# The mask and row-decay additions of a DeltaNet head's exponent table, moved from GpSimd to VectorE

## The reference

```
gc = cumsum(g)                                  # per chunk
decay[i, j] = exp(gc[i] - gc[j])  for j <= i,  else 0
lower = strict_tril(beta * (k k^T) * decay)
sol = inverse(I + lower) @ [v*beta, k*beta*exp(gc)]
qk = tril((q k^T) * decay)
per chunk: o = q_dec S + qk v_new ;  S = S*exp(g_last) + k_dec^T v_new
```

## Time and profile before

| | |
|---|---|
| median of the runs | 1423.48 us |
| the profiled execution's own time | 1425.28 us |
| its span | 1423.6 us |
| mean granted TensorE clock in it | 0.987 |
| PE busy | 94% of the span |
| DVE busy | 56% |
| ACT busy | 48% |
| POOL busy | 20% |

### The profile page before, as it was taken

How to read it: one execution, slowest core, us unless ns; L and a number is a source line. 1 busy time by engine, 2 the same in 40 slices (tenths; PEclk the granted TensorE clock), 3 DMA queues, 4 the chain that set the end, 5 groups by cost and what they waited for, 6 DMA issues and landing times.

```text
span 1423.6 us, 25677 instructions
## 1 busy us (share of the span) xinstructions
PE 1337.1 (94%) x9981; PEld 984.1 (69%) x9981; DVE 803.6 (56%) x2210; ACT 680.7 (48%) x1757; POOL 284.4 (20%) x206
## 2 busy tenths in 40 slices
PE   5999999999999998499999999999999999998998
PEld 4866766667544456388777877788778787875543
DVE  6235444444354426867578576675776775852243
ACT  6155464554555425246465463664654736543121
POOL 7211021110011143304122141131220413200000
PEclk9999999999999999799999999999999999999999
DMA  5011010020211111011021110110111101034121
GB/s 184 31 44 31 15 45 16 30 75 30 89 60 60 73 60 47 30 46 31 17 65 41 35 56 17 46 45 32 60 31 46 46 16 61 1 137 175 30 74 74
DMA packets 19416, 74.81 MB, mean 53 GB/s; under 512 B 3040, under 2 KB 3296, under 8 KB 17760
## 3 DMA queue, kind: packets, MB, share of 16 engines
q1 hardware_dynamic: 19296, 73.18, 15.0%
HBM read 61.04 MB, written 12.12 MB: 51 GB/s over the span
## 4 chain that ended last, share of the span: by engine, by line
PE 70%; DVE 14%; ACT 9%; issue 4%; DMA 2%; POOL 1%; SPq 0%; POOLq 0%; DVEq 0%; ACTq 0%
PE bank L1629 16%; PE bank L1726 12%; PE bank L1701 8%; PE bank L1766 4%; PE bank L1656 4%; PE bank L1682 3%; PE bank L1741 3%; PE bank L1667 3%; DVE arena L1531 2%; PE bank L1900 2%; PE bank L1914 2%; PE bank L1825 2%; PE bank L1917 2%; DVE arena L1391 2%; DVE arena L1533 2%
## 5 line engine op out<-in xcount | busy, mean ns | idle before, releaser
L1726 PE MATMUL bank<-hn_hi,w_hi 128*128 128x512 f32 x512 | 225.6, 441 | 17.5 <-ACT arena L1049 17.5
L1726 PE MATMUL bank<-hn_hi,w_lo 128*128 128x512 f32 x512 | 203.8, 398 | 0.0
L1726 PE MATMUL bank<-hn_lo,w_hi 128*128 128x512 f32 x512 | 203.0, 397 | 0.0
L1629 PE MATMUL bank<-hn_hi,w_hi 128*128 128x512 f32 x320 | 136.8, 428 | 0.5 <-ACT arena L984 0.3
L916 POOL TENSOR_TENSOR w_lo<-arena,w_hi 128x1024 fp32r<-128x1024 f32 x30 | 76.7, 2557 | 298.8 <-ACT w_hi L1080 298.8
L1629 PE MATMUL bank<-hn_hi,w_lo 128*128 128x512 f32 x320 | 125.9, 394 | 0.0
L1629 PE MATMUL bank<-hn_lo,w_hi 128*128 128x512 f32 x320 | 125.8, 393 | 0.0
L1726 PEld LDWEIGHTS bank<-hn_hi,w_hi 128*128 128x128 f32 x512 | 98.3, 192 | 36.4 <-ACT arena L1049 20.4
L1701 PE MATMUL bank<-arena 128*128 128x512 f32 x256 | 119.0, 598 | 0.0
L1726 PEld LDWEIGHTS bank<-hn_hi,w_lo 128*128 128x128 f32 x512 | 97.8, 191 | 22.7
L1263 DVE CUSTOM_DVE_ANT_0 arena<-bank,arena 128x384 f32<-128x384 f32 (+1 forms) x128 | 70.1, 582 | 67.0 <-issue 66.7
(11 more groups left out here) (231 smaller groups left out, 2670.8 us busy)
## 6 DMA issues: line engine op xcount, KB each, us to landing
arena<-in_w SPq DMA_DIRECT2D x52, 512.0 KB, 3.6
arena<-in_x SPq DMA_DIRECT2D x16, 512.0 KB, 4.5
arena<-gc_scratch SPq DMA_DIRECT2D x8, 1024.0 KB, 5.0
x_scratch<-arena SPq DMA_DIRECT2D x8, 512.0 KB, 2.6
arena<-x_scratch SPq DMA_DIRECT2D x8, 512.0 KB, 3.7
out<-arena SPq DMA_DIRECT2D x8, 512.0 KB, 2.6
oT_scratch<-arena SPq DMA_DIRECT2D x7, 512.0 KB, 4.9
arena<-oT_scratch SPq DMA_DIRECT2D x7, 512.0 KB, 8.1
```

The source lines that it names most:

```text
L1629: ins = te.matmul(bank[r % 2][:], wp[:, tile % 2, k], hp[:, k, hf * HALF:(hf + 1) * HALF], start=(k == 0 and m == 0), stop=(k == KT - 1 an ...
L1726: ins = te.matmul(b[:], wp[:, t % 2, k], hp[:, k, hf * HALF:(hf + 1) * HALF], start=(k == 0 and m == 0), stop=(k == KT - 1 and m == 2))
```

## The change

The event list stays as it is. The `etm` event is taken out of the POOL program and put into the DVE program. DVE executes the same two additions for each direction, in its own order, directly behind `tab1` and ahead of everything else that follows in the list. `link` makes the next DVE instruction wait for the completion of this one.

```diff
--- before.py
+++ after.py
@@ -914,13 +914,6 @@
                     t = e[1]
                     pool.wait_ge(w_rounded, t + 1)
                     gp.tensor_tensor(w_lo[:, t % 2], ring1[:, t % 2], w_hi[:, t % 2].bitcast(F32), ALU.subtract).then_inc(w_split, 1)
-                elif e[0] == "etm":
-
-                    h, d = e[1], e[2]
-                    pool.wait_ge(tab_dve, h * 3 + 1)
-                    gp.tensor_tensor(ET[:, d], ET[:, d], bc(emask[:, d], NT), ALU.add).then_inc(pch, 1)
-                    pool.wait_ge(pch, 8 + 2 * h + d)
-                    gp.tensor_tensor(ET[:, d], ET[:, d], bc(head_tab2[:, h % 2, 2, NT * d:NT * d + NT], P, 2), ALU.add).then_inc(et_masked, 1)
                 elif e[0] == "diag":
@@ -1376,6 +1369,12 @@
                     link(ve.memset(invT, 0.0))
+                elif e[0] == "etm":
+
+                    h, d = e[1], e[2]
+                    dve.wait_ge(tab_dve, h * 3 + 1)
+                    link(ve.tensor_tensor(ET[:, d], ET[:, d], bc(emask[:, d], NT), ALU.add))
+                    ve.tensor_tensor(ET[:, d], ET[:, d], bc(head_tab2[:, h % 2, 2, NT * d:NT * d + NT], P, 2), ALU.add).then_inc(et_masked, 1)
                 elif e[0] == "conv":
```

## The result

The changed kernel takes 1458.66 us (median of four runs, 1456.56 to 1459.61) against 1423.86 for the kernel before on the same chip. The ratio is 1.0238, with a 95% interval of 1.0217 to 1.0260. The change makes the kernel 34.8 us slower. The forecast was 1466, in a range of 1440 to 1473.

What follows compares the result with a forecast made beforehand. PE was taken to stall behind DVE's late gate eviction: 32.4 (PE's loss) + 10.2 (clock) + 0.8 (head 1) - 0.9 (head 0) = +42.5 us, giving 1466.0 for the median, range 1440 to 1473.

Steps and rivals of the forecast that it cites:

- What bounds: Behind the small table, DVE has 1.29 us of room before the gate eviction L1471, then PE's key transposes stop.
- Duration of the additions: Four 128x1024 additions per head on DVE, 1.22 us each, bounds 0.745 and 1.285.
- The collision: At the shared SBUF port POOL's L916 goes ahead of DVE's fourth addition, which ends at 928.07 instead of 925.85.
- the other order: DVE's fourth addition gets the port before POOL's L916; L1471 3.60 us late, total 1451; chance 0.27.
- What PE loses: Key transposes 5.82 us later, less 0.42 taken up at L1860 and L1818: 5.40 per head, 32.4 over six head changes.
- The clock: PE's granted clock falls behind each 6 us stall, costing 1.7 us at six heads, 10.2 in all.
- Head 0: DVE's constant chain: 4.85 of additions plus 1.3 of collision less 7.1 no longer lost to POOL's masks, -0.9 us.
- Head 1: No gate eviction; POOL goes before the third addition and the state copies reach PE's L1799 late, +0.8 us.
- DVE first at the port: Rival: the fourth addition precedes L916, 3.18 us net lost per head, clock falls at five of six; 1451; chance 0.27.
- The cheap case: Rival: additions of 0.745 us, giving 1429, or a held clock, giving 1443 or 1456; chance 0.13.
- The freed port: Rival: DVE no longer stands still behind POOL's masks, so the kernel gets faster, about 1419; chance 0.05.
- No change: Rival: the table is not on the bound path, delays are taken up before the inversion; 1423.5; chance 0.05.

Runs made afterwards that it cites:

- pool-waits kernel: Changed kernel, but POOL waits at each head until both directions are masked, so L916 cannot run beside the fourth addition; 1447.24 us, ratio 1.0161.
- 24 fillers: Changed kernel with 24 extra 128x128 matmuls, results unused, on PE ahead of the key transposes of heads 2 to 7; 1450.34 us, ratio 1.0180.
- 48 fillers: Changed kernel with 48 extra 128x128 matmuls, results unused, on PE ahead of the key transposes of heads 2 to 7; 1477.31 us, ratio 1.0369.
- woven: Changed kernel with DVE's additions placed one by one into gaps around the gate eviction and state copies, and POOL's L916 held back; 1421.85 us, ratio 0.9985.

## Why the prediction was right

*What bounds.* Shown. DVE's gate eviction became the wait in front of PE six times, and moving the additions behind it took four fifths of the loss away.

*Duration of the additions.* 1.22 was taken. Measured 1.22 (medians 1.224 and 1.225).

*The collision.* Predicted 3.4 for the fourth addition and L1470 "some 7 us behind the table"; measured 3.38 and 6.99. POOL won the port at each of the six heads, as the sum said with a margin of some 0.03. The sum took each addition from bounds of 0.745 to 1.285, so it couldn't decide an order by that margin; that it named the right one was luck. The prediction itself gave the other order 0.27. The pool-waits kernel priced the collision at 11.4 us in all.

*What PE loses.* Here two terms were mis-sized. The transposes were to be 5.82 later and are 5.51 later. In before they waited for ACT's silu, not for the eviction, which had some 0.2 of room, and the eviction moved by 5.70. And 0.42 was to be taken up behind them. The 24 fillers give 5.51 - (97.63 - 93.30) = 1.18, the 48 fillers 1.38. The two places were right and their sizes wrong: I had read the idle time of PE's matmuls there, 0.17 and 0.25, and not that of the weight loads ahead of them. These rows of before are the same instructions on PEld:

```profile
925.92 1.86 PEld L1860 LDWEIGHTS bank<-arena 128*128 128x128 f32 x16 [0.36 <-ACT arena L1101]
...
933.04 0.71 PEld L1818 LDWEIGHTS bank<-arena 128*128 128x128 f32 x4 [0.68 <-ACT arena L1066]
```

They sum to 1.04. Followed from matmul to matmul, from the table's start in before and in 24 fillers (the head at 920.78 and 930.27), PE's delay is 5.51 at the first key transpose and 5.69 at the fifth. It is 5.46 at the end of the first L1818 group, 5.03 two matmuls into L1860, and 4.41 behind the first matmuls of the next L1818. Then it stands at 4.33. Three other heads give the same as far as there.

*The clock.* It fell at all six heads. Priced at 1.7 from a window of before, measured at 1.48. The sum for one head is 5.51 - 1.18 + 1.48 = 5.81, the same as 99.11 - 93.30; it must be, since 1.18 and 1.48 were themselves got as differences of these periods. 7.1 was predicted. The 1.3 of difference over six heads is 7.8 us. In the profiled spans the difference is 31.2 where 42.5 was predicted, 11.3 less: about 7.8 from here, 2 from the last head and 1.2 from head 1. The medians are 34.8 apart, 3.6 more than the spans. No term of the sum foresaw that, and it brings the forecast that much nearer by luck.

*The last head.* Six heads were counted alike, but the last one gained back about 2 us: 226.56 - 222.82 = 3.74. In the final stretch of before the granted clock fell behind a 2.8 us stall; in after it stayed at 1.00 there. Before's row, and the one of after that answers to it, in windows of 5 us:

```profile
1295.00:1300.00 5.00, 5.00 (x18) 3.51 (x17) 1.50 (x2) 1.62 (x5) 0.00 (x0) 0.66 0.09 36
```

```profile
1327.00:1332.00 5.00, 5.00 (x25) 3.09 (x24) 1.67 (x4) 1.91 (x5) 0.00 (x0) 1.00 0.12 51
```

Whether this comes with the change or with the single execution is not shown. The grant falls at this place in eight of the ten kernels profiled, and not in after and in 24 fillers, the two whose transposes come 5.51 late. On the other side, the profiled execution of after is the fastest of its four, with a mean granted clock of 0.977 where the others have 0.973 and 0.974.

*Heads 0 and 1.* Head 0 was -0.9 and is -0.9: DVE's constant chain ends 1.2 earlier in after, in spite of 4.9 us of additions in front (L1444 at 573.30, against 574.49 in the earlier trace rows). Head 1 was +0.8 and is -0.4. POOL did go before the third addition, but the relief of DVE's later taps (L1390 took 1.27 there, and L1391 in before 3.30) outweighed the late state copies. The table shows both: 91.77 and 91.76 in the pool-waits and woven kernels, where the state copies are not late, so the relief is 0.5 and the late copies cost 0.1. The relief was left out of this term of the prediction, and the cost was put at 0.8.

*The rivals.* DVE first at the port: the pool-waits kernel is that case, at 1447 where I said 1451. The cheap case fell with the durations and the clock. The freed port is real but small at heads 0 and 1, and was not on the path elsewhere. No change: excluded by the interval.

## What to carry to other kernels

- Ask of moved work what is queued behind it and how much room stands in front of that. Here 1.29 us of gap and about 1.2 us of slack behind PE were free. The other 4.3 us per head were paid in full, with 1.5 for the clock on top. The same 32 additions cost 34.8 us in one place and nothing in another.
- When an engine is taken off a job, what it does next starts earlier. Compute when, and whether that meets the moved work at a shared port; a wait that keeps the old order won back a third of the loss.
- Where PE waits, read the weight load's row beside the matmul's. Here the waits of the two came to 1.04 and 0.42 at the same places, and the first was nearer to the slack that the runs showed.
- Look in the trace for one instruction of a group that takes ten times its siblings' time while POOL runs. One such row per head, on the path, was worth 0.75% of the kernel.

## What the runs showed of the hardware

- A DVE addition of two SBUF tensors and a POOL instruction that reads SBUF did not overlap, they went one behind the other: 3.38 us for an addition of 1.22, when POOL had started 0.04 earlier. Whoever asked first went first. POOL was first at six heads alike; at head 1 of after DVE had started 0.66 earlier, and POOL's L916 took 2.79 instead of 2.34.
- A form with one SBUF tensor was held up too: L1389 (128x1024) took 1.54 in before at 926.00, beside POOL's L921, against a median of 0.745.
- A gate eviction that reads one PSUM and one SBUF tensor wasn't held up: in the pool-waits kernel the pair L1473 took 1.40 with L916 beside it, as without it.
- The granted clock fell to 0.50 behind each stall of 5.9 us, fell too behind the 3.8 us stalls of the pool-waits kernel (0.50 and 0.97 in two windows of 3 us behind one, 0.50 and 0.57 behind another), and stayed at 1.00 where PE was fed with matmuls of no use. Feeding PE was worth 1.48 us per head.
- An f32 matmul of 128x128 by 128x128 took 0.22 us of PE's time, as two instructions.
